# Moving weights of the token-major products, stored and read in descending column order

## The chip, the cores and the metric

The kernel runs on one core of a Trainium2 chip. A core has TensorE (matmuls), VectorE, ScalarE and GpSimd, a queue for transfers (SyncE), a memory on the chip (SBUF) and accumulators for the matmuls (PSUM, eight banks of 512 fp32 columns here). A matmul keeps one operand in the array, the stationary one, 128 x 128 here, and streams the other, the moving one, through it, column by column. The metric is the device time of one execution in microseconds (us); lower is better.

## The reference

Two transformer blocks in fp32, the first of two layers, the second of one, on 256 tokens of width 2048 (the second block with 16 more, so-called meta tokens). What matters here are the large products with weights, and above all those of the feed-forward parts:

```python
D_MODEL = 2048; SEQ = 256; D_FF = 4 * D_MODEL
for l in range(DEPTH):                      # first block, DEPTH = 2
    h = rms_norm(x, attn_norm[l])
    proj = h @ w_in[l]
    ...                                     # three attention mixers
    mixed = jnp.concatenate([out_a, out_b, out_c], axis=-1)
    x = x + mixed @ w_o[l]
    h = rms_norm(x, mlp_norm[l])
    x = x + jnp.square(jax.nn.relu(h @ w_up[l])) @ w_down[l]
...
    # second block, one layer
    h_res = h_res + mix @ w_out[l]
    h2 = _rmsnorm(h_res, norm_mlp_g[l])
    h_res = h_res + jnp.square(jax.nn.relu(h2 @ w_up[l])) @ w_down[l]
```

## The kernel before

All weights lie in one array in memory, `stream`, in the order in which they are used, in chunks of 2 MB (`P` = 128 rows of `CE` = 4096 fp32 values). SyncE's queue brings them into two buffers `raw`. Each is halved into tiles, and each tile is split by two engines: ScalarE writes a rounded copy `w_hi` (type fp32r, which TensorE multiplies in a single pass), VectorE writes the rest `w_lo` = `raw` - `w_hi`. There are two `w_hi` and two `w_lo`. The activations are split in the same way (`xg`, and `act_hi` with `act_lo`), and a product is the sum of three: high by high, high by low, low by high.

Two kinds of products follow each other on TensorE.

- Channel-major ones (`tile`, by `paired_row` or `row_with_meta`): a 128 x 128 block of the weights is stationary and the activations of 256 tokens move. `paired_row` does with one matmul of 512 columns, two runs of 256 that lie apart in `xg`, what needs `w_hi`, and with a second one of 256 columns what needs `w_lo`. The up projections are done so.
- Token-major ones (`wide`, `last_wide`, `wide_values`, `out_half`): 128 tokens of the activations are stationary, and 512 columns of the weights move (`W` = 512), a row `[:, i, :]` of the views `wide_hi` and `wide_lo`. Each step over 128 input channels is three matmuls of 512 columns for each of the two groups of 128 tokens (`m`). The sums stay in PSUM banks as tokens by channels, and are added to the residual `x` (line 1772). The down projections, the two output projections and the values of two attention mixers are done so.

The feed-forward part goes in four quarters: `ups` makes 2048 hidden channels (512 matmuls), then `widened` multiplies them by their part of the down weights, 4 column groups `c` x 4 tiles `t` x 4 rows `i` x 2 `m` x 3 = 384 matmuls. The host function `wide_chunks` lays out the weights of the down projections and the values, `half_chunks` those of the output projections.

The order of the work is written out by hand, with semaphores between the engines: `lo_ready` tells TensorE that a half of a tile is split, `tile_done` tells ScalarE that a tile may be written over. The loops over the quarters and layers are loops on the chip. In the names of a trace's matmul, the moving operand stands first: `bank<-w_hi,act_lo` has moving weights, `bank<-xg,w_hi` moving activations.

Of the kernel before, what the change touches and what calls it, by code (L numbers as in the profile page):

```python
# [23 lines left out]
P = 128  # L24
D = 2048
KT = D // P
# [56 lines left out]
CE = KT * CW  # L83
W = 512
NC = D // W
# [42 lines left out]
def build(nc, stream, params, tables, tables2, cbias, xrow, gfin, metaT, smat, out, stabs, urow, yrow):  # L128
# [197 lines left out]
    with ExitStack() as ctx:  # L326
        bank = [ctx.enter_context(nc.psum_tensor(f"bank{i}", [P, 512], F32)) for i in range(8)]
# [199 lines left out]
        def pair_free(T, c):  # L527

            return evacuated(T - 3) if c == 0 else evacuated(T - 5)
# [8 lines left out]
        def lo_count(T, half):  # L538
            return 2 * T + half + 9
# [127 lines left out]
        def _(pe):  # L667
            pe.sem_inc(tile_done, 2)

            def mm(o, a, b, start, stop):  # L670
                return pe.matmul(o, a, b, start=start, stop=stop, skip_group_check=True)  # L671
# [13 lines left out]
            def tile(T, b, j, before=None, free=None, row=paired_row, counts=1):  # L685

                pe.wait_ge(evac_done, evacuated(T - 4) if free is None else free)
                for h in range(2):
                    pe.wait_ge(lo_ready, lo_count(T, h))
                    for k in range(8 * h, 8 * h + 8):  # L690
                        if before is not None:
# [4 lines left out]
            wide_hi, wide_lo = ([v[j][:].rearrange("p k n -> p (k n)").rearrange("p (k n) -> p k n", n=W) for j in range(2)]  # L696
                                for v in (hi, lo))

            def last_wide(T, c, k0):

                for m in range(2):
                    for i in range(4):
                        if m == 0 and i % 2 == 0:
                            pe.wait_ge(lo_ready, lo_count(T, i // 2))
                        k = (k0 + 12 + i) % KT
                        o = bank[2 * (c % 2) + m][:]
                        a_hi, a_lo = (v[:, k, P * m:P * m + P] for v in (act_hi, act_lo))
                        mm(o, a_hi, wide_hi[1][:, i, :], False, False)
                        mm(o, a_hi, wide_lo[1][:, i, :], False, False)
                        last = mm(o, a_lo, wide_hi[1][:, i, :], False, i == 3)  # L710
                    last.then_inc(tile_done, 1)

            def wide(T, c, t, k0, before=None):

                if t == 0:
                    pe.wait_ge(evac_done, pair_free(T, c))
                for i in range(4):
                    if i % 2 == 0:
                        pe.wait_ge(lo_ready, lo_count(T, i // 2))
                    k = (k0 + 4 * t + i) % KT  # L720
                    if before is not None and c == 0:
                        before(k)
                    for m in range(2):
                        o = bank[2 * (c % 2) + m][:]
                        a_hi, a_lo = (v[:, k, P * m:P * m + P] for v in (act_hi, act_lo))
                        mm(o, a_hi, wide_hi[t % 2][:, i, :], t == 0 and i == 0, False)
                        mm(o, a_hi, wide_lo[t % 2][:, i, :], False, False)
                        last = mm(o, a_lo, wide_hi[t % 2][:, i, :], False, t == 3 and i == 3)
                last.then_inc(tile_done, 1)

            def wide_values(T, t, free):

                def row(i, m):

                    k = 4 * t + i
                    x_hi, x_lo = (xg[:, e, k, META + P * m:META + P * m + P] for e in range(2))
                    mm(bank[m][:], x_hi, wide_hi[t % 2][:, i, :], k == 0, False)
                    mm(bank[m][:], x_hi, wide_lo[t % 2][:, i, :], False, False)
                    return mm(bank[m][:], x_lo, wide_hi[t % 2][:, i, :], False, k == KT - 1)

                pe.wait_ge(lo_ready, lo_count(T, 0))
                for m in range(2):
                    if t == 0:
                        pe.wait_ge(evac_done, free[m])
                    for i in range(2):
                        row(i, m)
                pe.wait_ge(lo_ready, lo_count(T, 1))
                for i in (2, 3):
                    for m in range(2):
                        last = row(i, m)  # L750
                last.then_inc(tile_done, 1)

            def out_half(T, t, h, b, k0, free=None):

                def row(i, m):

                    k = k0 + 4 * t + i
                    o = bank[b + m][:]
                    a_hi, a_lo = (v[:, k, P * m:P * m + P] for v in (act_hi, act_lo))
                    mm(o, a_hi, wide_hi[t][:, i, :], t == 0 and i == 0, False)  # L760
                    mm(o, a_hi, wide_lo[t][:, i, :], False, False)
                    return mm(o, a_lo, wide_hi[t][:, i, :], False, t == 1 and i == 3)

                pe.wait_ge(lo_ready, lo_count(T, h))
                if free is not None:
                    for m in range(2):
                        pe.wait_ge(evac_done, free - 1 + m)
                        for i in (2 * h, 2 * h + 1):
                            row(i, m)
                    return  # L770
                for i in (2 * h, 2 * h + 1):
                    for m in range(2):
                        last = row(i, m)
                if h == 1:
                    last.then_inc(tile_done, 1)
# [27 lines left out]
            def widened(Tb, k0, n=None, before=None, tables=None):  # L803

                for c in range(NC):
                    for t in range(4):
                        if n is None and tables is END and c == NC - 1 and t == 3:
                            last_wide(Tb + 4 * c + t, c, k0)
                            break
                        wide(Tb + 4 * c + t, c, t, k0, before)  # L810
                        if n is not None and c and t == 0:
                            if c == 1 and tables is not None:
                                pe.wait_ge(tabs_out, tables)
                            pe.wait_ge(evac_done, evacuated(Tb + 4 * c - 1))
                            turn_x(n, c - 1)
# [1852 lines left out]

def wide_chunks(w):

    return w.reshape(2, 8, P, -1, W).transpose(3, 0, 2, 1, 4).reshape(-1, P, CE)


def half_chunks(w):

    return w.reshape(2, 8, P, NC, W).transpose(0, 3, 2, 1, 4).reshape(-1, P, CE)


def by_channel(v, axis):
# [6 lines left out]
def ffn_chunks(up, down):  # L2686
    f = D
    return [c for i in range(FCH) for c in (chunks(up[:, f * i:f * i + f]), wide_chunks(down[f * i:f * i + f]))]


def weight_stream(a):
    parts = []
    r0, rh = Q_RANK + KV_RANK, A_ROPE // 2
    for l in range(DEPTH):
        w = a["w_in"][l]
        rotary = np.tile(w[:, r0:r0 + A_ROPE], (1, 2))
        qb, kb, vb, qc, kc, vc = np.split(w[:, r0 + A_ROPE:], 6, 1)
        parts += [chunks(np.concatenate([w[:, :r0], qb, kb], 1)), wide_chunks(vb), chunks(np.concatenate([qc, kc], 1)), wide_chunks(vc),
                  chunks(np.concatenate([rotary, np.zeros((D, P), np.float32)], 1))]
        w = a["w_uq"][l].reshape(Q_RANK, HA, A_NOPE + A_ROPE)  # L2700
        halves = [w[:, :, A_NOPE + rh * e:A_NOPE + rh * e + rh].reshape(Q_RANK, -1) for e in range(2)]
        w = np.concatenate(halves + [w[:, :, :A_NOPE].reshape(Q_RANK, -1)], 1)
        kv = a["w_ukv"][l].reshape(KV_RANK, HA, A_NOPE + A_V)
        parts += [latent_chunk(w[:, 768:], kv[:, :, :A_NOPE]), latent_chunk(w[:, :768], kv[:, :, A_NOPE:]), np.zeros((1, P, CE), np.float32)]
        parts.append(half_chunks(np.roll(a["w_o"][l], -1024, axis=0)))
        parts += ffn_chunks(a["w_up"][l], a["w_down"][l])
    w = a["w_in_2"][0]
    q, k, v, u = np.split(w, [W2, W2 + KV2 * HD2, W2 + 2 * KV2 * HD2], 1)
    parts += [chunks(by_channel(u, 1)), chunks(k), chunks(v), chunks(q)]
    parts.append(by_channel(by_channel(a["w_glu_2"][0], 0), 1).reshape(T2, P, 2, 512).transpose(2, 1, 0, 3).reshape(2, P, CE))  # L2710
    w = np.concatenate([by_channel(a["w_out_2"][0][W2:], 0), a["w_out_2"][0][:W2]], 0)
    parts.append(half_chunks(w))
    parts += ffn_chunks(a["w_up_2"][0], a["w_down_2"][0])
    s = np.concatenate(parts, 0)
    assert s.shape[0] == C_ALL
    return s
# [113 lines left out]
```

## Time and profile before

| | us |
|---|---|
| median of 3 runs | 3118.84 |
| lowest and highest run | 3118.07, 3119.42 |
| span of the profiled execution | 3119.2 |
| TensorE busy in it | 3099.6 (99%) |
| VectorE busy | 1839.2 (59%) |
| ScalarE busy | 1465.8 (47%) |
| GpSimd busy | 719.0 (23%) |

The profiled execution is within 0.4 us of the median, so its rows can be added up against the measured time as they are. Matmuls overlap in the records: one begins while the one before it drains. What a matmul costs is therefore the distance from its start to the next start, and not the length of its record.

### The profile page before, as it was taken

How to read it: one execution, taken by the hardware profiler on the slowest of the kernel's cores; microseconds unless marked ns; L12 is line 12 of the kernel's file. 1: busy time of each engine (PE TensorE's matmuls, PEld its weight loads, DVE VectorE, ACT ScalarE, POOL GpSimd, SP SyncE). 2: the span in 40 equal slices, each digit the busy share in tenths (PEclk: the TensorE clock that was granted, in tenths of full speed). 3: DMA queues.
4: the chain of work that ended last, by engine and by line, in shares of the span. 5: the costliest groups of instructions: out<-in, count | busy, mean ns of one | idle time of the engine just before them, and what ended most of it. 6: DMA issues, size and time to landing. Idle time of an engine off the chain costs nothing.

```text
span 3119.2 us, 45296 instructions
## 1 busy us (share of the span) xinstructions
PE 3099.6 (99%) x16368; PEld 2659.7 (85%) x16368; DVE 1839.2 (59%) x2369; ACT 1465.8 (47%) x2274; POOL 719.0 (23%) x746
## 2 busy tenths in 40 slices
PE   8999999999999999999999999999999999999999
PEld 7888888888888888888888888889888888888887
DVE  5676655555555567665555555567686555555554
ACT  5454544444345545454453444552565434444443
POOL 1422241231411143042314150115030101001010
PEclk9999999999999999999999999999999999999999
DMA  6534565655655554455556465657433555555554
GB/s 241 189 142 164 189 219 189 219 189 188 219 189 211 192 187 152 164 182 213 192 188 219 185 219 189 224 213 275 171 120 142 189 199 189 195 192 188 189 188 162
DMA packets 66640, 598.04 MB, mean 192 GB/s; under 512 B 14320, under 2 KB 24816, under 8 KB 31424
## 3 DMA queue, kind: packets, MB, share of 16 engines
q1 hardware_dynamic: 54912, 588.17, 51.7%
q10 hardware_dynamic: 11184, 5.49, 0.7%
q0 software_dynamic: 400, 2.44, 0.2%
q8 instruction: 91, 1.49, 0.2%
q14 instruction: 53, 0.43, 0.0%
HBM read 577.93 MB, written 18.15 MB: 191 GB/s over the span
## 4 chain that ended last, share of the span: by engine, by line
PE 95%; DVE 2%; DMA 1%; ACT 1%; issue 1%; ACTq 0%; DVEq 0%
PE bank L671 93%; DMA urow<-us 1%; PE bank L783 1%; DVE w_lo L1723 1%; PE bank L942 0%; ACT w_hi L1209 0%; PE bank L831 0%; DVE sb L2243 0%; DMA par<-params 0%; DMA u<-urow 0%; DVE w_lo L1717 0%; DVE gbuf L2208 0%; DVE ks L2186 0%; ACT act_hi L1559 0%; DVE act_lo L2216 0%
## 5 line engine op out<-in xcount | busy, mean ns | idle before, releaser
L671 PE MATMUL bank<-xg,w_hi 128*128 128x512 f32 (+1 forms) x4256 | 1434.4, 385 | 1.7 <-issue 1.7
L671 PE MATMUL bank<-xg,w_lo 128*128 128x256 f32 (+1 forms) x4064 | 1142.8, 281 | 0.0
L671 PEld LDWEIGHTS bank<-xg,w_hi 128*128 128x128 f32 x4256 | 789.6, 188 | 168.4 <-issue 2.3
L1717 DVE TENSOR_TENSOR w_lo<-raw,w_hi 128x1024 fp32r<-128x1024 f32 x512 | 668.1, 1341 | 439.4 <-ACT w_hi L1220 439.1
L1220 ACT ACTIVATE w_hi<-raw 128x1024 fp32r<-128x1024 f32 x512 | 514.0, 1052 | 634.4 <-PE bank L671 634.4
L671 PEld LDWEIGHTS bank<-xg,w_lo 128*128 128x128 f32 x4064 | 765.4, 188 | 0.9
L671 PE MATMUL bank<-w_hi,act_hi 128*128 128x512 f32 x1920 | 752.5, 392 | 0.2 <-issue 0.2
L671 PE MATMUL bank<-w_hi,act_lo 128*128 128x512 f32 x1920 | 747.7, 389 | 0.0
L671 PE MATMUL bank<-w_lo,act_hi 128*128 128x512 f32 x1920 | 747.2, 389 | 0.0
L1723 DVE TENSOR_TENSOR w_lo<-raw,w_hi 128x1024 fp32r<-128x1024 f32 x510 | 626.0, 1234 | 170.4 <-ACT w_hi L1209 169.4
L1209 ACT ACTIVATE w_hi<-raw 128x1024 fp32r<-128x1024 f32 x514 | 514.4, 1052 | 174.8 <-PE bank L671 147.6
L2517 POOL TENSOR_TENSOR act_lo<-hid,act_hi 128x256 f32 x192 | 193.6, 1009 | 1459.1 <-ACT act_hi L1260 1459.1
L671 PEld LDWEIGHTS bank<-w_hi,act_lo 128*128 128x128 f32 x1920 | 360.4, 188 | 75.6
L671 PEld LDWEIGHTS bank<-w_hi,act_hi 128*128 128x128 f32 x1920 | 360.5, 188 | 73.7 <-issue 0.3
L671 PEld LDWEIGHTS bank<-w_lo,act_hi 128*128 128x128 f32 x1920 | 360.6, 188 | 73.1
L1796 DVE TENSOR_TENSOR hid<-bank,hid 128x256 f32<-128x256 f32 x192 | 81.4, 424 | 371.4 <-ACT hid L1249 371.4
L1249 ACT ACTIVATE hid<-bank 128x256 f32<-128x256 f32 x192 | 73.5, 383 | 401.6 <-PE bank L671 401.6
L1260 ACT ACTIVATE act_hi<-hid 128x256 f32 (+1 forms) x192 | 80.3, 418 | 145.2 <-DVE hid L1806 145.2
L1772 DVE SCALAR_TENSOR_TENSOR x<-bank,stats,x 128x512 f32<-128x512 f32 x96 | 67.8, 747 | 92.6 <-issue 77.5
L671 PE MATMUL bank<-w_hi,xg 128*128 128x512 f32 x256 | 82.3, 396 | 0.0
L1806 DVE SCALAR_TENSOR_TENSOR hid<-hid 128x256 f32<-128x256 f32 x192 | 80.4, 419 | 0.0
L2586 POOL TENSOR_TENSOR xgf<-x,gfb 128x512 f32<-128x512 f32 x16 | 30.9, 1950 | 125.4 <-DVE x L1772 109.1
(346 smaller groups left out, 2014.9 us busy)
## 6 DMA issues: line engine op xcount, KB each, us to landing
raw<-stream SPq DMA_DIRECT2D x260, 2048.0 KB, 7.7
stabs<-ssm_tabs SPq DMA_DIRECT2D x8, 1176.0 KB, 9.7
rdo<-stabs SPq DMA_DIRECT2D x8, 768.0 KB, 7.3
ssm_bc<-smat SPq DMA_DIRECT2D x8, 640.0 KB, 11.7
raw<-stream SPq DMA_DIRECT2D x4, 1024.0 KB, 8.6
stabs<-ssm_f SPq DMA_DIRECT2D x8, 512.0 KB, 10.8
drv<-stabs SPq DMA_DIRECT2D x8, 512.0 KB, 5.6
trig<-stabs SPq DMA_DIRECT2D x8, 408.0 KB, 5.9
```

The source lines that it names most:

```text
L671: return pe.matmul(o, a, b, start=start, stop=stop, skip_group_check=True)
L783: last = pe.transpose(bank[4 + k % 4][:, P * m:P * m + P], x[:, m, P * k:P * k + P], ident)
L1209: act.activation(hi[j][:, 8 * h:8 * h + 8, :], raw[r][:, 8 * h:8 * h + 8, P * j:P * j + P], ACT.Copy)\
L1220: act.activation(flat_hi[j][:, 1024 * h:1024 * h + 1024], flat_raw[r][:, 2048 * j + 1024 * h:2048 * j + 1024 * h + 1024], ACT.Copy).then_i ...
L1249: act.activation(dst, bank[b][:, S:2 * S], ACT.Copy).then_inc(low_out, counts)
L1260: act.activation(act_hi[:, bass.ds(4 * q + t, 1), :], hid[t][:].rearrange("p (a n) -> p a n", a=1), ACT.Copy)\
L1717: dve.tensor_tensor(flat_lo[j][:, 1024 * h:1024 * h + 1024], flat_raw[r][:, 2048 * j + 1024 * h:2048 * j + 1024 * h + 1024], flat_hi[j][:, ...
L1723: dve.tensor_tensor(lo[j][:, 8 * h:8 * h + 8, :], raw[r][:, 8 * h:8 * h + 8, P * j:P * j + P], hi[j][:, 8 * h:8 * h + 8, :].bitcast(F32), ...
L1772: dve.scalar_tensor_tensor(out=one, in0=bank[2 * (c % 2) + m][:], scalar=rs2[:, m:m + 1], in1=one, op0=ALU.mult, op1=ALU.add).then_inc(eva ...
L1796: return dve.tensor_tensor(dst, bank[b][:, 0:S], dst, ALU.add).then_inc(folded, counts)
L1806: dve.scalar_tensor_tensor(out=one, in0=one, scalar=0.0, in1=one, op0=ALU.max, op1=ALU.mult).then_inc(evac_done, 1)
L2517: pool.tensor_tensor(act_lo[:, bass.ds(4 * q + t, 1), :], hid[t][:].rearrange("p (a n) -> p a n", a=1), act_hi[:, bass.ds(4 * q + t, 1), : ...
```

## The change

The host functions write each group of 512 weight columns back to front, and the matmuls of the four token-major functions read the row of 512 with a step of -1, from its last element to its first. So column n of the product is what it was and goes where it went. Nothing else is changed: the three products, their order, the stationary operands, the output columns in PSUM, the splits (which take the elements in ascending order as they lie) and the transfers (the same bytes in the same shapes). Each engine's instructions are the same in number and order; of the moving operands of these matmuls, start address and step differ.

```diff
@@ last_wide (wide, wide_values and out_half in the same way) @@
-                        mm(o, a_hi, wide_hi[1][:, i, :], False, False)
-                        mm(o, a_hi, wide_lo[1][:, i, :], False, False)
-                        last = mm(o, a_lo, wide_hi[1][:, i, :], False, i == 3)
+                        w_hi, w_lo = (v[1][:, i, ::-1] for v in (wide_hi, wide_lo))
+                        mm(o, a_hi, w_hi, False, False)
+                        mm(o, a_hi, w_lo, False, False)
+                        last = mm(o, a_lo, w_hi, False, i == 3)
...
 def wide_chunks(w):
 
-    return w.reshape(2, 8, P, -1, W).transpose(3, 0, 2, 1, 4).reshape(-1, P, CE)
+    return w.reshape(2, 8, P, -1, W)[..., ::-1].transpose(3, 0, 2, 1, 4).reshape(-1, P, CE)
 
 
 def half_chunks(w):
 
-    return w.reshape(2, 8, P, NC, W).transpose(0, 3, 2, 1, 4).reshape(-1, P, CE)
+    return w.reshape(2, 8, P, NC, W)[..., ::-1].transpose(0, 3, 2, 1, 4).reshape(-1, P, CE)
```

## Rows read from the trace of the kernel before

**Rows 1.** The page: busy time of each engine, its share, its instructions.

```profile
PE 3099.6 (99%) x16368; PEld 2659.7 (85%) x16368; DVE 1839.2 (59%) x2369; ACT 1465.8 (47%) x2274; POOL 719.0 (23%) x746
```

**Rows 2.** The page: chain that ended last, by engine, in shares of the span.

```profile
PE 95%; DVE 2%; DMA 1%; ACT 1%; issue 1%; ACTq 0%; DVEq 0%
```

**Rows 3.** Groups by line and shape: busy us, mean ns; idle before.

```profile
L671 PE MATMUL bank<-w_hi,act_hi 128*128 128x512 f32 x1920 | 752.5, 392 | 0.2 <-issue 0.2
L671 PE MATMUL bank<-w_hi,act_lo 128*128 128x512 f32 x1920 | 747.7, 389 | 0.0
L671 PE MATMUL bank<-w_lo,act_hi 128*128 128x512 f32 x1920 | 747.2, 389 | 0.0
L671 PE MATMUL bank<-w_hi,xg 128*128 128x512 f32 x256 | 82.3, 396 | 0.0
L671 PE MATMUL bank<-w_lo,xg 128*128 128x512 f32 x128 | 50.3, 393 | 0.0
```

**Rows 4.** Windows, a down and an up quarter: stretch, its us, PE busy, clock, DMA share, GB/s.

```profile
2499.30:2586.20 86.90, 86.90 (x385) 1.00 0.53 194
2586.20:2675.60 89.40, 89.40 (x514) 1.00 0.51 188
```

**Rows 5.** TensorE's timeline in that quarter: start us, duration us, instruction.

```profile
2582.71 0.39 PE L671 MATMUL bank<-w_hi,act_lo 128*128 128x512 f32 x1
2582.93 0.39 PE L671 MATMUL bank<-w_hi,act_hi 128*128 128x512 f32 x1
...
2586.11 0.39 PE L671 MATMUL bank<-w_hi,act_lo 128*128 128x512 f32 x1
2586.34 0.40 PE L671 MATMUL bank<-xg,w_hi 128*128 128x512 f32 x1
```

**Rows 6.** TensorE's timeline, last of the 256 steps of the following up quarter.

```profile
2675.36 0.39 PE L671 MATMUL bank<-xg,w_hi 128*128 128x512 f32 x1
2675.59 0.28 PE L671 MATMUL bank<-xg,w_lo 128*128 128x256 f32 x1
```

**Rows 7.** TensorE's timeline, products of the GLU: single runs of 256 columns.

```profile
2261.79 0.28 PE L671 MATMUL bank<-act_lo,w_hi 128*128 128x256 f32 x1
...
2264.91 0.28 PE L671 MATMUL bank<-act_hi,w_hi 128*128 128x256 f32 x1
```

**Rows 8.** TensorE's timeline in layer 1: plain fp32, 512 moving columns (line 905).

```profile
204.87 1.88 PE L671 MATMUL bank<-raw,proj 128*128 128x512 f32 x4
```

**Rows 9.** Groups by line and shape: all such records.

```profile
L671 PE MATMUL bank<-raw,proj 128*128 128x512 f32 x16 | 7.5, 593 | 0.0
```

**Rows 10.** ScalarE's timeline in a down quarter: splits of one tile, idle before.

```profile
2504.99 2.01 ACT L1220 ACTIVATE w_hi<-raw 128x1024 fp32r<-128x1024 f32 x2 [2.11 <-PE bank L671]
2510.38 2.01 ACT L1220 ACTIVATE w_hi<-raw 128x1024 fp32r<-128x1024 f32 x2 [3.37 <-PE bank L671]
```

**Rows 11.** VectorE's timeline in the same place.

```profile
2506.09 2.36 DVE L1717 TENSOR_TENSOR w_lo<-raw,w_hi 128x1024 fp32r<-128x1024 f32 x2 [2.51 <-ACT w_hi L1220]
2511.47 2.36 DVE L1717 TENSOR_TENSOR w_lo<-raw,w_hi 128x1024 fp32r<-128x1024 f32 x2 [3.02 <-ACT w_hi L1220]
```

**Rows 12.** The page: the weights' transfers, KB each, median us to landing.

```profile
raw<-stream SPq DMA_DIRECT2D x260, 2048.0 KB, 7.7
```

More of the change, by code:

```diff
@@ L725, in wide @@
                         a_hi, a_lo = (v[:, k, P * m:P * m + P] for v in (act_hi, act_lo))
-                        mm(o, a_hi, wide_hi[t % 2][:, i, :], t == 0 and i == 0, False)
-                        mm(o, a_hi, wide_lo[t % 2][:, i, :], False, False)
-                        last = mm(o, a_lo, wide_hi[t % 2][:, i, :], False, t == 3 and i == 3)
+                        w_hi, w_lo = (v[t % 2][:, i, ::-1] for v in (wide_hi, wide_lo))
+                        mm(o, a_hi, w_hi, t == 0 and i == 0, False)
+                        mm(o, a_hi, w_lo, False, False)
+                        last = mm(o, a_lo, w_hi, False, t == 3 and i == 3)
                 last.then_inc(tile_done, 1)
@@ L736, in row @@
                     x_hi, x_lo = (xg[:, e, k, META + P * m:META + P * m + P] for e in range(2))
-                    mm(bank[m][:], x_hi, wide_hi[t % 2][:, i, :], k == 0, False)
-                    mm(bank[m][:], x_hi, wide_lo[t % 2][:, i, :], False, False)
-                    return mm(bank[m][:], x_lo, wide_hi[t % 2][:, i, :], False, k == KT - 1)
+                    w_hi, w_lo = (v[t % 2][:, i, ::-1] for v in (wide_hi, wide_lo))
+                    mm(bank[m][:], x_hi, w_hi, k == 0, False)
+                    mm(bank[m][:], x_hi, w_lo, False, False)
+                    return mm(bank[m][:], x_lo, w_hi, False, k == KT - 1)
                 pe.wait_ge(lo_ready, lo_count(T, 0))
@@ L759, in row @@
                     a_hi, a_lo = (v[:, k, P * m:P * m + P] for v in (act_hi, act_lo))
-                    mm(o, a_hi, wide_hi[t][:, i, :], t == 0 and i == 0, False)
-                    mm(o, a_hi, wide_lo[t][:, i, :], False, False)
-                    return mm(o, a_lo, wide_hi[t][:, i, :], False, t == 1 and i == 3)
+                    w_hi, w_lo = (v[t][:, i, ::-1] for v in (wide_hi, wide_lo))
+                    mm(o, a_hi, w_hi, t == 0 and i == 0, False)
+                    mm(o, a_hi, w_lo, False, False)
+                    return mm(o, a_lo, w_hi, False, t == 1 and i == 3)
                 pe.wait_ge(lo_ready, lo_count(T, h))
```

## The prediction

> **What bounds the kernel now.** I read the page first, for who is busy, then the chain that ended last, then the groups of matmuls by shape, and last TensorE's timeline, for the distance from one start to the next. TensorE is busy for 99% of the span, 3099.6 of 3119.2 us [rows 1], and 95% of the chain that ended last is its work [rows 2]. So any time that the changed matmuls gain or lose reaches the end one for one, and nothing that another engine gains does. The span is 0.4 us from the median of the runs (3118.84), so sums against the span hold for the median too.
>
> The changed matmuls are those whose moving operand is `w_hi` or `w_lo` and whose stationary one is an activation. There are 3 x 1920 with `act_hi` or `act_lo`, and 256 + 128 with `xg`: 6144 in all, each of 512 columns [rows 3]. Their records are 389 to 396 ns long, but they overlap. From the start at 2582.71 to that at 2586.11 there are 15 steps, all without a wait: 3.40 / 15 = 226.7 ns for each [rows 5]. A whole down quarter of 384 such matmuls lasts 86.9 us at a granted clock of 1.00, which is the level of 2.4 GHz [rows 4]; 86.9 / 384 = 226.3 ns, the same within the rounding of the edges. So the change touches 6144 x 0.2267 = 1393 us, 45% of the span, and 1 ns more or less on each is 6.1 us, 0.2% of the time. That is also about the smallest difference that a measurement of this kernel can tell from no change.
>
> Of the 226.7 ns, 512 columns at one a cycle of 2.4 GHz take 213.3, and 13.3 are left. The same remainder shows at half the width: 26 steps of 256 columns from 2261.79 to 2264.91 are 120.0 ns each [rows 7], and 256 columns take 106.7. So what a matmul costs here is one cycle a column, plus 13.3 ns whatever its width. A descending read can change either: the rate, or the fixed part.
>
> **The change part by part.** The host's new layout costs nothing on the chip: the transfers keep their 2048 KB each [rows 12], and what value lies at an address is nothing to a copy or a subtraction. The two splits of a tile read and write in ascending order as before, and their instructions are the same. They have room as well: for one tile TensorE takes 24 x 226.7 ns = 5.4 us, ScalarE 2.01 and VectorE 2.36, and ScalarE stands idle for 3.37 us before the next tile until TensorE has freed one [rows 10, 11]. If the matmuls ran without the 13.3 ns, a tile would take 5.1 us, and this cover would still hold. The stationary operand, its load, the order on the queue, the semaphores and the ascending columns in PSUM stay, and no instruction is added. So all of the change lies in one thing: how fast TensorE takes 512 fp32r columns that come with a step of -1. No matmul of the trace reads in descending order, so this price must be bounded.
>
> From near: the up projection's matmul of 512 columns is made of two runs of 256 that lie apart. A pair of it and a matmul of 256 columns takes (2675.36 - 2586.34) / 255 = 349.1 ns [rows 5, 6]. Taking 120.0 for the narrow one [rows 7] leaves 229.1 for the wide one, 2.4 more than for one run of 512. So leaving the ascending row in the middle of a matmul costs 2.4 ns at most, and I take that as the price if a descending read makes the unit that generates addresses do anything special once per matmul: 6144 x 2.4 ns = 15 us. The largest fixed price that I allow is that the 13.3 ns come twice, 6144 x 13.3 ns = 82 us, and the largest gain is that they go, also 82 us; nothing in the trace says what they are, so a gain is not excluded.
>
> From afar: if the rate changes, the nearest row is the plain fp32 product with 512 moving columns. Four records take 1.88 us, the last one 593 ns long [rows 8, 9], so they start (1.88 - 0.593) / 3 = 0.429 us apart, 0.84 ns a column: half the rate of fp32r in one record. Line 905 is run eight times and leaves 16 records [rows 9], two for each matmul, so a plain fp32 matmul costs 858 ns in all. The bounds of the unknown step are thus -13.3 ns and +631 ns, from -82 us to +3880 us.
>
> I take **zero**. An operand row of 512 fp32r values is the same set of addresses from either end, neighbours stay neighbours, and an even count that begins at the row's last element also leaves every aligned pair or group of four whole. The trace shows that crossing to another run costs next to nothing (2.4 ns), so the address side is no bottleneck, and this row is nearer to the change than the plain fp32 one, which differs in type. A sum of zero leaves 3119.2 us against the span, 3118.8 against the median; I say 3119.0.
>
> [...] The 512 columns of a changed matmul are 128 x 512 x 4 = 262,144 bytes, and in 226.7 ns that is 1156 GB/s [rows 5], while the plain fp32 product takes the same bytes at 611 GB/s [rows 8]. [...]
>
> **The rivals.** *Half rate (slower).* fp32r takes twice as many bytes per unit of time as a plain fp32 pass. If it does so by fetching two ascending neighbours at once, and a step of -1 breaks the pairs, the 512 columns come one by one, as in plain fp32: 429 ns in place of 226.7. The place is the intake of the moving operand, the price (429 - 226.7) x 6144 = 1243 us, and it decides as soon as the pairing asks for a step of exactly +1. The time would be 4362 us; the 19.6 us in which TensorE is idle now [rows 1] could hide no more than that. For it: the factor of two between the types is there in the rows. Against it: in a descending row the pairs are as whole as in an ascending one. I give it 13%. A worse form of it, in which the matmul is done as plain fp32 in both of its passes, costs 631 ns each and gives 6999 us; 3%, since type and record count of the instruction don't change.
>
> *A fixed price per matmul (slower).* Something is done once for each matmul with a descending row. At 2.4 ns this is 3134 us, at the full 13.3 ns 3201. For it: the two-run matmuls are indeed a little dearer. Against it: GLU and wide products have the same fixed part at different widths, so nothing in it seems to come from the shape. 11%.
>
> *A gain.* The 13.3 ns are partly a matter of how the moving stream meets the load of the next stationary operand, and reading from the other end avoids it. Half of it gone gives 3119 - 41 = 3078, all of it 3037. Nothing in the rows speaks for it. 6%.
>
> That the change doesn't do what it says, because the descending step is lost on the way to the instruction, would give the same time as my forecast, and no row would tell the two apart.
>
> **How the numbers follow.** No measurable change 67%, half rate 13%, plain fp32 3%, fixed price 11%, gain 6%. The likeliest gives 3119.0. The range takes in the whole fixed price, up to 3201, and the gain up to its half, down to 3078. Left out are the 16% of the two changed rates and some 3% of the gain. Faster by over 0.2% is the gain, 6%; within 0.2%, 67%; slower by over 0.2%, 13 + 3 + 11 = 27%. The distribution is lopsided: if I am wrong, the likeliest error is a very large one.
>
> **What would show it.** If I am right, the five groups with moving weights keep mean lengths of 389 to 396 ns, starts in a down quarter stay 226 to 227 ns apart, and the quarter lasts 86.9 us. With half rate the starts lie 429 ns apart, a quarter lasts 165 us, ScalarE's idle time before each split grows by some 4.9 us, the up quarters stay at 89.4 us [rows 4], and TensorE's busy share stays at 99%. With a fixed price all the starts move by one small amount, 229 to 240 ns, and the quarter lasts 88 to 92 us; then the same product with narrower rows would lose the same nanoseconds per matmul. I am wrong by a mechanism that I did not see if the quarters with moving activations change, or if the granted clock leaves 1.00.

## The result, and the profile after

The change makes the kernel slower: 3157.03 us (median of 4 runs, 3150.83 to 3158.17) against 3118.8 us (4 runs), a ratio of 1.0119 with a 95% interval of 1.0107 to 1.0131. That is 38 us where I had forecast none. It lies inside the range, on the side of the second rival, a price per matmul, which I had given 11%.

The page of the kernel after has the same numbers of instructions as [rows 1]; TensorE alone is busy for longer, by 37.2 us, and its share of the chain is 96% (95% in [rows 2]):

```profile
span 3155.8 us, 45296 instructions
PE 3136.8 (99%) x16368; PEld 2660.8 (84%) x16368; DVE 1836.1 (58%) x2369; ACT 1464.3 (46%) x2274; POOL 713.9 (23%) x746
PE 96%; DVE 2%; DMA 1%; ACT 1%; issue 0%; ACTq 0%; DVEq 0%
```

The span grew by 36.6 us. The groups by line and shape show where. All five groups of [rows 3] have longer records, by 4 to 8 ns, and the channel-major ones beside them (moving `xg`), which the change leaves alone, keep theirs (1358.3 us and 394 ns before for the one of 512 columns):

```profile
L671 PE MATMUL bank<-w_hi,act_hi 128*128 128x512 f32 x1920 | 767.9, 400 | 0.2 <-issue 0.2
L671 PE MATMUL bank<-w_hi,act_lo 128*128 128x512 f32 x1920 | 763.0, 397 | 0.0
L671 PE MATMUL bank<-w_lo,act_hi 128*128 128x512 f32 x1920 | 763.0, 397 | 0.0
L671 PE MATMUL bank<-w_hi,xg 128*128 128x512 f32 x256 | 83.3, 401 | 0.0
L671 PE MATMUL bank<-w_lo,xg 128*128 128x512 f32 x128 | 50.8, 397 | 0.0
L671 PE MATMUL bank<-xg,w_hi 128*128 128x512 f32 x3872 | 1357.1, 394 | 1.4 <-issue 1.4
```

TensorE's timeline of a down quarter answers to [rows 5]. Both rows below are first matmuls of a step, and 360 matmuls lie between their starts: 84.00 / 360 = 233.3 ns, against 226.7 before. The stretch has the granted clock of 1.00 that it had in [rows 4], the level of 2.4 GHz, and TensorE is never idle in it:

```profile
2528.58 0.40 PE L671 MATMUL bank<-w_hi,act_hi 128*128 128x512 f32 x1
...
2612.58 0.40 PE L671 MATMUL bank<-w_hi,act_hi 128*128 128x512 f32 x1
...
2525.00:2614.30 89.30, 89.30 (x386) 1.00 0.52 190
```

So the price in the down projections is 6.7 ns a matmul. For all 6144 that would be 41.0 us, and the sum below is 3.4 us less. Nearly half of that lies in the values (stationary `xg`), whose 384 distances grew by 2.7 ns in the mean and not by 6.7; most of what remains lies in the output projections (some 5.7 ns each). Before, 51 starts of the values took 11.77 us, 230.8 ns each, 4 ns more than in a down quarter:

```profile
91.61 0.39 PE L671 MATMUL bank<-w_lo,xg 128*128 128x512 f32 x1
...
103.38 0.39 PE L671 MATMUL bank<-w_lo,xg 128*128 128x512 f32 x1
```

After, 48 starts take 11.20 us, 233.3 ns, as in a down quarter:

```profile
91.89 0.40 PE L671 MATMUL bank<-w_lo,xg 128*128 128x512 f32 x1
...
103.09 0.40 PE L671 MATMUL bank<-w_lo,xg 128*128 128x512 f32 x1
```

Added up over the whole trace, the distances that begin with a changed matmul sum to 1401.9 us before and 1439.5 after, 37.6 more; all others together differ by 1.3 us. In dense stretches the descending row is uniform, and what it costs depends on how well the ascending one did in its place.

### The profile page after: what moved, and what is told of

Read it like the earlier page. It is cut to its first block, busy times and chain, and to the rows that moved or that the text cites. A ratio compares the mean times of both kernels' runs of the same rounds, so it can differ in the third digit from the quotient of the medians.

```text
span 3155.8 us, 45296 instructions
## 1 busy us (share of the span) xinstructions
PE 3136.8 (99%) x16368; PEld 2660.8 (84%) x16368; DVE 1836.1 (58%) x2369; ACT 1464.3 (46%) x2274; POOL 713.9 (23%) x746
## 3 DMA queue, kind: packets, MB, share of 16 engines
q10 hardware_dynamic: 11184, 5.49, 0.7%
## 4 chain that ended last, share of the span: by engine, by line
PE 96%; DVE 2%; DMA 1%; ACT 1%; issue 0%; ACTq 0%; DVEq 0%
PE bank L671 95%; PE bank L787 1%; DMA urow<-us 1%; PE bank L946 0%; DVE w_lo L1727 0%; PE bank L835 0%; DMA u<-urow 0%; DMA par<-params 0%; DVE sb L2247 0%; DVE w_lo L1721 0%; DVE gbuf L2212 0%; ACT w_hi L1213 0%; DVE ks L2190 0%; ACT act_hi L1563 0%; DVE act_lo L2220 0%
## 5 line engine op out<-in xcount | busy, mean ns | idle before, releaser
L671 PE MATMUL bank<-w_hi,act_hi 128*128 128x512 f32 x1920 | 767.9, 400 | 0.2 <-issue 0.2
L671 PE MATMUL bank<-w_lo,act_hi 128*128 128x512 f32 x1920 | 763.0, 397 | 0.0
L671 PE MATMUL bank<-w_hi,act_lo 128*128 128x512 f32 x1920 | 763.0, 397 | 0.0
```

## The experiments

The first ten kernels put several directions or orders into one execution: the down projections go in four groups of 512 weight columns, written out one after the other, and each gets its own. A pair of rows per group, 72 matmuls apart if not said otherwise, gives the distance. The scatter between executions doesn't touch such a comparison. The output is the reference's unless a text says otherwise.

### Which order costs

```diff
+READ = [(1, 512, 1, 1), (1, 512, -1, -1), (128, 4, -1, 1), (128, 4, 1, -1)]
+                a, b, blocks, within = READ[c]
...
+                return v[:, i, :].rearrange("p (a b) -> p a b", b=b)[:, ::blocks, ::within]
```

> The kernel before, with only the down projections changed, and each of their four groups of 512 weight columns read in another order, stored so that the product is the same. Group 0: ascending. Group 1: descending, as in the change. Group 2: 128 blocks of 4 columns, last block first, ascending inside a block. Group 3: blocks ascending, the 4 columns inside a block descending. Measured is the distance between the starts of consecutive matmuls, group by group in one execution. Theory A (what costs is the long way down through memory, whatever the order inside 16 bytes): group 0 226.7 ns, group 1 233.3, group 2 233.3 or more, group 3 226.7. Theory B (what costs is a step of -1 between neighbours): group 2 226.7, group 3 233.3 or much more. If both patterns with two dimensions cost far more than 233 ns, then short runs are dear for a reason of their own. The whole takes 3118.8 + 4608/4 x 6.7 ns = 3126.5 us for group 1 alone, and as much again for each other group that costs.

Measured, group by group, 226.7, 233.3, 233.3 and 226.7 ns; in all 3127.9 us against 3113.96, in single runs. The timeline of groups 2 and 3 (starts 16.80 and 16.32 us apart):

```profile
2547.99 0.40 PE L671 MATMUL bank<-w_hi,act_hi 128*128 128x512 f32 x1
...
2564.79 0.40 PE L671 MATMUL bank<-w_hi,act_hi 128*128 128x512 f32 x1
...
2570.33 0.39 PE L671 MATMUL bank<-w_hi,act_hi 128*128 128x512 f32 x1
...
2586.65 0.39 PE L671 MATMUL bank<-w_hi,act_hi 128*128 128x512 f32 x1
```

Theory A holds, B falls. A step of -1 inside 4 columns (16 bytes) is free; going down from one such block to the next costs the whole 6.7 ns, even though the columns inside ascend. The fear of the first rival, pairs of neighbours that a negative step takes apart, has no ground here.

### Whether the start address costs

```diff
-    hi = [place(f"w_hi{i}", [P, KT, P], F32R) for i in range(2)]
+    hi = [place(f"w_hi{i}", [P, KT * P + 8], F32R)[:, 1:1 + KT * P].rearrange("p (k n) -> p k n", n=P) for i in range(2)]
```

> The kernel before with the two tiles w_hi laid 4 and 36 bytes past a multiple of 64 (the w_lo tiles stay on one), and in the down projections column groups 0 and 2 read ascending, 1 and 3 descending. A descending read of an aligned row starts at its last element, 4 bytes before a boundary; of a shifted row it starts on a boundary, and it is now the ascending read that starts 4 bytes off. Theory C (what costs is a start that isn't the first element of an aligned group): descending w_hi go back to 226.7 ns, ascending w_hi rise to 233.3, w_lo stay at 226.7 ascending and 233.3 descending. Theory A or B (direction itself): w_hi ascending 226.7 and descending 233.3 wherever the row starts. The whole: by theory C 3119 + (1152 x 2 of w_lo and w_hi mixed) about 3134 us, by A or B about the same, so only the distances tell.

Ascending 234.3 ns (16.87 us for 72), descending 235.6 (16.96 us):

```profile
2534.55 0.40 PE L671 MATMUL bank<-w_hi,act_hi 128*128 128x512 f32 x1
...
2551.42 0.40 PE L671 MATMUL bank<-w_hi,act_hi 128*128 128x512 f32 x1
...
2557.05 0.40 PE L671 MATMUL bank<-w_hi,act_hi 128*128 128x512 f32 x1
...
2574.01 0.40 PE L671 MATMUL bank<-w_hi,act_hi 128*128 128x512 f32 x1
```

Theory C falls, since no descending row came back to 226.7. Neither did what A or B foretold come: with this layout the ascending ones lose 7.6 ns and nearly the whole difference is gone. That is not the price of the 4 bytes alone. The wider tiles also push what lies behind them, the `w_lo` tiles and the activations, 64 bytes further on, and the run on alignment below shows that such a shift by itself costs ascending rows up to 7 ns. In all 3167.26 us against 3113.96, so this layout costs more than the change did. The distances that begin with a token-major matmul sum to 1449.1 us, 47.2 more than in the kernel before, and all others to 1706.1, against 1707.0. So the shifted tiles cost the channel-major products, whose stationary operands they are, nothing. The other 6 us fit the granted clock of the two executions (0.999 here, 1.000 in the 3113.96), of which the last experiment tells more.

### Whether the price is fixed or goes with the width

```diff
+                n, step = WIDTH[c], READ[c][2]          # WIDTH = [256, 256, 128, 128]
+                for j in range(W // n):
+                    at = W - n - n * j if step < 0 else n * j
```

> The kernel before with the down projections' matmuls cut into narrower ones, the product the same: column group 0 two of 256 ascending, group 1 two of 256 descending, group 2 four of 128 ascending, group 3 four of 128 descending. If the price of descending is fixed per matmul (6.7 ns): 256 columns take 120.0 ascending and 126.7 descending; 128 columns take 6.7 more descending as well, unless the load of the stationary operand is by then the longer part (records of 188 ns that overlap), which hides it. If it goes with the number of columns (6.7 ns on 512): 120.0 and 123.3, and 1.7 more at 128.

Here the output is not the reference's after all: the first matmul of each narrow piece starts the sums of its bank anew, so the pieces beside it lose that step. The work on TensorE is the same. 256 columns take 120.0 ns ascending (17.28 us for 144) and 118.3 descending (17.04 us):

```profile
2856.61 0.28 PE L671 MATMUL bank<-w_hi,act_hi 128*128 128x256 f32 x1
...
2873.89 0.28 PE L671 MATMUL bank<-w_hi,act_hi 128*128 128x256 f32 x1
...
2879.62 0.28 PE L671 MATMUL bank<-w_hi,act_hi 128*128 128x256 f32 x1
...
2896.66 0.28 PE L671 MATMUL bank<-w_hi,act_hi 128*128 128x256 f32 x1
```

At this width the descending row is the faster one, by 1.7 ns, which neither theory allows. At 128 columns both take 111.7 ns, so something else bounds them. From 256 and 512 columns I drew two new lines, and had them tested at other widths:

```diff
+            CUT = [(0, 384), (0, 384), (0, 320), (0, 320)]
...
+                for j, (p, n) in enumerate(((0, cut), (cut, W - cut))):
```

> As x3, with uneven cuts and the product the same: down projections' column groups 0 (ascending) and 1 (descending) in pieces of 384 and 128 columns, groups 2 (ascending) and 3 (descending) in pieces of 320 and 192. From x3 and the groups of 512, two lines: ascending a fixed 13.3 ns and 0.4167 ns a column, so 384 columns 173.3 and 320 columns 146.7 ns; descending a fixed 3.3 ns and 0.4492 ns a column (the price is in the rate: 5.2 ns on 160 columns), so 384 columns 175.8 and 320 columns 147.1 ns. If instead descending is a fixed 20.0 ns a matmul and 256 columns were an exception: 180.0 and 153.3 ns.

The distances depend on the neighbours (a matmul of 384 that follows one of 128 begins 226.6 to 230.6 ns before the next, the two after it 174 to 180), so only the mean over a whole step of six is clean: 143.9 ns ascending and 144.4 descending with pieces of 384 and 128, 128.9 and 130.0 with 320 and 192. Per 512 columns, three matmuls of each width in a step of six, that is 1.1 and 2.2 ns more for descending: less than at 512 undivided, more than at 256 twice (-3.3). Neither a fixed sum nor a rate gives this row of numbers. But the pieces of 128 and 192 columns may themselves be bounded by what gave 111.7 ns at 128, which could hide a part of the price. So the two lines are not borne out, and this run alone doesn't refute them; that the sign turns at 256 is what speaks against a fixed sum and against a lower rate.

### Whether each descending matmul pays for itself

```diff
+            STEPS = [(-1, 1, 1), (1, -1, 1), (-1, -1, 1), (1, 1, 1)]
```

> The kernel before with part of the three matmuls of a step in the down projections reading their row descending, and the layout unchanged, so those read mirrored columns and the output isn't the reference's. Group 0: only the first (w_hi with act_hi) descending. Group 1: only the second (w_lo). Group 2: the first two. Group 3: none. If each descending matmul pays for itself, 6.7 ns lie on each distance that begins or ends with one: per three matmuls 686.7, 686.7, 693.3 and 680.0 ns. If a change of direction is what costs, group 2 costs as much as groups 0 and 1, and a row of three descending ones would cost nothing, which the changed kernel already speaks against (233.3 each).

Per three matmuls: 693.3, 686.7, 703.3 and 680.0 ns (starts 16.64, 16.48, 16.88 and 16.32 us apart for 72). Groups 0 and 2:

```profile
2510.79 0.39 PE L671 MATMUL bank<-w_hi,act_hi 128*128 128x512 f32 x1
...
2527.43 0.39 PE L671 MATMUL bank<-w_hi,act_hi 128*128 128x512 f32 x1
...
2555.01 0.39 PE L671 MATMUL bank<-w_hi,act_hi 128*128 128x512 f32 x1
...
2571.89 0.39 PE L671 MATMUL bank<-w_hi,act_hi 128*128 128x512 f32 x1
```

Only the second and the fourth came as expected. One descending matmul costs 6.7 or 13.3 ns depending on its place among the three, and two cost 23.3, more than three do in the changed kernel (20.0). The prices don't add up; the matmuls are not independent of each other.

### How the block size enters

The same kernel as the first, with `READ = [(32, 16, 1, -1), (8, 64, 1, -1), (2, 256, 1, -1), (2, 256, -1, 1)]`.

> As x1, with other sizes of block. Down projections, column group 0: blocks of 16 columns ascending, descending inside a block; group 1: blocks of 64, the same; group 2: two halves of 256, the lower first, descending inside each; group 3: the upper half first, ascending inside each. Theory F (a fixed price for starting at the far end of a long way down): groups 0 and 3 226.7 ns, 1 between, 2 233.3 or twice the price. Theory L (the moving row and the load of the next stationary operand, which runs beside it, meet on the same part of SBUF for longer when the row goes down): the price depends on how the first columns run, since the load covers the first part of the stream: group 0 226.7, groups 1 and 2 near 233.3, group 3 226.7 or less.

Groups 1, 2 and 3 take 233.3, 233.3 and 226.7 ns: a downward stretch of 64 columns is as dear as one of 512, and taking the upper half first is free. Group 0, downward stretches of 16 columns, takes 266.7 ns (19.20 us for 72), 40 more than ascending:

```profile
2541.52 0.43 PE L671 MATMUL bank<-w_hi,act_hi 128*128 128x512 f32 x1
...
2560.72 0.43 PE L671 MATMUL bank<-w_hi,act_hi 128*128 128x512 f32 x1
```

Theory F fits groups 2 and 3, but had less than 233.3 for group 1 and 226.7 for group 0; L, which fits 1 to 3, had 226.7 for group 0 too. By neither would the shortest stretches be the dearest. No other order of the same 512 columns costs as much, and I have no explanation for it. It also gives the kernel's time: 3180.46 us against 3119.13.

### Whether output order or other steps cost

```diff
+                if c == 0:
+                    o = o[:, ::-1]
+                if c == 1:
+                    o, w_hi, w_lo = o[:, ::-1], w_hi[:, ::-1], w_lo[:, ::-1]
+                if c >= 2: # a step of 2 over rows i and i + 1; c == 3: from the end
```

> The kernel before, with in the down projections: group 0 the output row in PSUM written descending, the moving row ascending; group 1 both descending (the same product as before); group 2 the moving row taken with a step of +2 over two rows of the tile; group 3 the same with a step of -2. In groups 0, 2 and 3 columns are mixed up, so the output isn't the reference's. If only the direction of the moving read costs: group 0 226.7 ns, group 1 233.3. If the order of the output costs as well, both rise. For a step of 2, four bytes of every eight: 226.7 if the rate holds, about 440 if only what lies in 8 neighbouring bytes can be fetched at once; descending then a little more than ascending, or the same.

Groups 0 and 1 take 226.7 and 233.3 ns: writing a row of PSUM from its end costs nothing, alone or together. Steps of +2 and -2 take 453.3 (32.64 us for 72) and 466.7 ns (33.60 us), each exactly twice its neighbour with a step of 1:

```profile
2901.09 0.63 PE L671 MATMUL bank<-w_hi,act_hi 128*128 128x512 f32 x1
...
2933.73 0.63 PE L671 MATMUL bank<-w_hi,act_hi 128*128 128x512 f32 x1
...
2944.77 0.65 PE L671 MATMUL bank<-w_hi,act_hi 128*128 128x512 f32 x1
...
2978.37 0.65 PE L671 MATMUL bank<-w_hi,act_hi 128*128 128x512 f32 x1
```

So the half rate of my first rival does exist. It comes when every second column is left out, and with 3654.99 us it is the disaster that I had feared. Whether what is fetched at once is 8 bytes or 16 this step doesn't tell: half of either is wasted. The Trainium skill's page "SBUF — State Buffer", in "Door 1: The DMA port swizzle (why `[64,N]` ≈ `[32,N]`)", has lines of 16 bytes in SBUF, which agrees with the free reversal inside four columns; its claim that fp32 may stride up to such a line for free does not agree with these 453.3 ns for a step of 8 bytes.

### Whether the stationary operand has a part in it

```diff
+            SHIFT = [(0, 4), (8, 16), (32, 48), (64, 96)]
+                        s = SHIFT[i][m]
+                        a_hi, a_lo = (v[:, k, s:s + P] for v in (act_hi, act_lo))
```

> The kernel before, groups 0 and 2 of the down projections ascending, 1 and 3 descending, and the stationary operand begins 0, 16, 32, 64, 128, 192, 256 or 384 bytes further on, by row i and token group m, so it holds other tokens in part and the output isn't the reference's. Theory L (the load of the stationary operand collides with the moving row): the distances change with this shift, ascending from 226 up to 237 as for the products with xg, whose stationary operands begin at changing multiples of 64 bytes, and descending as well. Theory F (a fixed price of a descending row): 226.7 and 233.3 ns for every shift.

Both theories are half right. Ascending rows are no longer 226.7 ns apart but 224 to 237.6, in the mean 231.9 (16.70 us for 72). Descending ones keep 233.3 (16.80 us) for every shift:

```profile
2562.16 0.39 PE L671 MATMUL bank<-w_hi,act_hi 128*128 128x512 f32 x1
...
2578.86 0.39 PE L671 MATMUL bank<-w_hi,act_hi 128*128 128x512 f32 x1
...
2584.44 0.40 PE L671 MATMUL bank<-w_hi,act_hi 128*128 128x512 f32 x1
...
2601.24 0.40 PE L671 MATMUL bank<-w_hi,act_hi 128*128 128x512 f32 x1
```

Then I took work away from the load:

```diff
+            COLS_IN = [64, 64, 32, 32]
+                p, a_hi, a_lo = o[0:n], a_hi[:, 0:n], a_lo[:, 0:n]
```

> The kernel before, with a narrower stationary operand in the down projections: 64 of its 128 columns in groups 0 (ascending) and 1 (descending), 32 in groups 2 (ascending) and 3 (descending). The other tokens are left out, so the output isn't the reference's. Theory L: with half the load or less there is less to collide with: the distances fall below 226.7 ns and the difference between the directions shrinks to 0 to 3 ns; with 32 columns it is nearly gone. Theory F: 6.7 ns between the directions at either width.

The load's records shrink from 188 to 135 and 108 ns, and nothing is gained. Ascending takes 230.0 ns with 64 columns and 231.7 with 32 (16.56 and 16.68 us for 72), more than with 128; descending takes 233.3 with either. If the descending row were slow since it collides with the load, a load of a quarter of the columns should have made it faster. Theory L falls as the cause of the 233.3 ns. What the load has a say in is the 226.7.

### Whether the 226.7 ns are a matter of alignment

One `w_hi` tile, both `w_lo` and all that lies behind them 64 bytes further on:

```diff
-    hi = [place(f"w_hi{i}", [P, KT, P], F32R) for i in range(2)]
+    hi = [place(f"w_hi{i}", [P, KT * P + 16 * (1 - i)], F32R)[:, 0:KT * P].rearrange("p (k n) -> p k n", n=P) for i in range(2)]
```

> The kernel before with one of the two w_hi tiles, both w_lo tiles and all behind them laid 64 bytes further on, and column groups 0 and 2 of the down projections ascending, 1 and 3 descending, the product the same. The activations are shifted by the same 64 bytes, so between w_hi of even tiles and activations the distance is another, and between odd ones it is the same. Theory P (the 226.7 ns of the ascending row are a favourable alignment of moving and stationary operand, lost when one shifts against the other; 233.3 is what a descending row takes wherever all lies): even tiles of groups 0 and 2 rise to 229 to 236 ns on w_hi, odd ones stay at 226.7, groups 1 and 3 stay at 233.3. If ascending is simply 226.7 at any multiple of 64 bytes, groups 0 and 2 stay at 226.7 throughout.

Over 72 starts ascending takes 231.5 and 231.3 ns in groups 0 and 2 (16.67 us in group 0), descending 233.3 (16.80 us):

```profile
2520.40 0.40 PE L671 MATMUL bank<-w_hi,act_hi 128*128 128x512 f32 x1
...
2537.07 0.39 PE L671 MATMUL bank<-w_hi,act_hi 128*128 128x512 f32 x1
...
2542.59 0.40 PE L671 MATMUL bank<-w_hi,act_hi 128*128 128x512 f32 x1
...
2559.39 0.40 PE L671 MATMUL bank<-w_hi,act_hi 128*128 128x512 f32 x1
```

These 72 mix even and odd tiles, of 24 matmuls each. The next rows are the starts of tiles 1, 2 and 3 of group 0 and the end of tile 3; they lie 5.49, 5.61 and 5.48 us apart, which is 228.5 ns a matmul in the odd tiles and 233.8 in the even one:

```profile
2523.21 0.39 PE L671 MATMUL bank<-w_hi,act_hi 128*128 128x512 f32 x1
...
2528.70 0.39 PE L671 MATMUL bank<-w_hi,act_hi 128*128 128x512 f32 x1
...
2534.31 0.39 PE L671 MATMUL bank<-w_hi,act_hi 128*128 128x512 f32 x1
...
2539.79 0.39 PE L671 MATMUL bank<-w_hi,act_hi 128*128 128x512 f32 x1
```

Theory P holds in the main. In the even tiles, where `w_hi` is shifted against `w_lo` and the activations, ascending loses its whole lead (233.2 to 233.8 ns in the mean of a tile), and descending stays. It does not hold in the detail, for the odd tiles, whose distance to the activations was unchanged, rose too (227.6 to 228.5 ns).

### The change in two parts

Down projections alone, by the change's own edit of `wide`, `last_wide` and the layout of their weights:

> The change in the down projections alone (4608 of the 6144 matmuls); values and output projections are as before. If each of them pays its own 6.6 ns and nothing else in the program answers: 4608 x 6.57 = 30 us, ratio 1.0097. If part of the change's cost comes from elsewhere, the two parts don't add up to the whole (1.0119).

Measured 3143.76 us (5 runs) against 3119.34 (15 runs): ratio 1.0083, 1.0069 to 1.0097. The other two functions alone:

> The change in the other 1536 matmuls alone, the values (384) and the output projections (1152). Their starts before lie 230.8 and some 227.8 ns apart by the trace, and 233.5 after, so 384 x 2.7 + 1152 x 5.6 = 7.5 us, ratio 1.0024; with a flat 6.67 ns each it would be 10.2 us, 1.0033. With x11 the sum should be 37 to 38 us.

Measured 3125.92 us (11 runs) against the same: 1.0027, 1.0016 to 1.0037. The two make 1.0110, the whole 1.0119 with an interval of 1.0107 to 1.0131. By the distances that begin with a changed matmul, summed over each trace, the parts cost 30.1 and 7.6 us, and the whole 37.6. So the parts add up, and nothing else in the program answers to the change.

That the first ratio lies below its 1.0097 has another cause. Its profiled execution is 3140.3 us long, 21.1 more than the kernel before, while its changed matmuls take 30.1 more. The windows between 2130 and 2160 us show the missing part. First the kernel before, then this one:

```profile
2130.00:2160.00 30.00, 28.64 (x202) 0.83 0.75 245
```

```profile
2130.00:2160.00 30.00, 29.77 (x248) 1.00 0.91 325
```

At the start of the second block, with short idle times of TensorE, the granted clock falls for a while in some executions and stays at 1.00 in others, and this moves the time by some 9 us: all distances that don't begin with a changed matmul sum to 1707.0 us in the first and 1697.9 in the second. The kernel before itself ran in 3110.97 to 3122.37 us. The two profiled executions of the result both have the fall (1707.0 and 1705.8 us), so their comparison is free of it. Single runs can't be compared to better than that, distances inside a quarter can.

## Why the prediction was right or wrong

**What bounds the kernel** was right. TensorE sets the end, and 37.6 us of longer matmuls came out as 36.6 of span.

**Layout, transfers, splits, other engines: zero.** Right: the unchanged matmuls sum to the same within 1.3 us.

**The price of a descending row: zero.** This is the step that failed. It is 6.7 ns in the down projections, and 37.6 / 6144 = 6.1 ns in the mean. I argued that the same addresses are read, that pairs and fours stay whole, and that a jump inside a row costs 2.4 ns at most. The first two are true, and the runs even confirm them: reversal inside 16 bytes and the upper half first cost nothing. None of it bears on the order in which the 16-byte blocks come, and this is what costs.

**"One cycle a column, plus 13.3 ns whatever its width"** was read from two kinds of matmul that happened to leave the same remainder, and taken for a property of the matmul. The remainder moves with the place of the operands: it is some 20 ns in the even tiles of the run with 64 bytes between them, for the same ascending 512 columns. The trace had the sign of it: among the groups of [rows 3] those with stationary `xg` had longer records (396 and 393 ns), and their starts were 230.8 ns apart. I used these groups for the count alone. Had I laid them beside the 226.7, I would have seen that the same ascending row of 512 columns has no one price, and would have put the fixed-price case near the forecast.

**The rivals.** *Half rate* did not come, for the reason given against it; its premise is real, as a step of 2 shows. *A fixed price* came true in sign and size: 6.1 ns lies between its 2.4 and its 13.3, and the time between its 3134 and 3201. The test that I named for it, the same loss at narrower rows, did not: at 256 columns the loss is a gain of 1.7 ns. *A gain* did not come at 512, and its mechanism, avoiding the load of the stationary operand, has no support in the run with a narrow load.

**The chances.** 67% for no measurable change leaned on one argument about addresses, for a reading order of which the trace had no row at all. The bounds were far apart, and the range held because the fixed price was taken whole. That the measured time lies inside it is luck and no merit of the argument: the case that the sum was built on did not come, and the one that did had 11%.

**What stays open.** Shown is: in a dense stretch the descending read of 512 columns takes 233.3 ns wherever moving and stationary operand lay at multiples of 16 bytes or more. The ascending one takes 226.7 when both lie as in the down projections, and 227.6 to 233.8, in the mean of a tile, in the other places tried. Not shown is why. Neither a fixed price for the start, nor a lower rate, nor the load of the stationary operand explains all the rows, and the 266.7 ns for descending stretches of 16 columns contradict the first two outright. An order in which the parts of SBUF come by turns, in which ascending rows fit and descending ones don't, would be my guess; no run tested it.

None of the versions beats the kernel before: no distance at 512 columns came below its 226.7 ns in the mean.

## What to carry to other kernels

For a moving operand of 512 fp32r columns, the order is free inside 16 bytes, and so is taking the upper half before the lower; going down from one 16 bytes to the next is not. Let the layout in memory follow the order in which the array reads, ascending, and turn the output round in PSUM if something must be turned. Keep moving and stationary rows at the alignment that a dense stream has shown to be good, since 64 bytes between them (up to 7.1 ns on 226.7), or tiles that begin 4 bytes off in a layout shifted by 64 (7.6 ns), cost as much as the wrong direction. Before a cost per matmul is called fixed, compare the start distances of all groups of the same width in the trace; where they differ, the remainder is a matter of place and can move with any edit that moves a buffer.

## What the runs showed of the hardware that I had not expected

- Descending fp32r rows of 512 columns start 233.3 ns apart, ascending ones 226.7, and of 256 columns 118.3 and 120.0: the sign turns with the width.
- Downward stretches of 16 columns with ascending blocks: 266.7 ns. Stretches of 4: 226.7. Stretches of 64, 256, 512: 233.3.
- A step of 2 elements doubles the time exactly, in both directions: 453.3 and 466.7 ns.
- A narrower stationary operand (64 or 32 columns for 128) makes ascending matmuls slower, 230.0 and 231.7 ns, not faster.
- Ascending rows lose their whole lead, 233.2 to 233.8 ns, where one of the operands is moved 64 bytes against the others.
- PSUM can be written from the end of a row at no cost (226.7 ns ascending, 233.3 descending, as without it).
- One descending matmul among three costs 6.7 or 13.3 ns depending on its place, and two cost 23.3, more than three.
